# Expert outputs of a two-layer decoder on one Trainium2 core: interleaved activation parts, descending weights and PSUM columns

## The reference

```python
def block(xb):
    q = (xb @ w_pq).reshape(PEER_BLOCK, P_HEADS, 2, P_HALF)
    sc = jnp.einsum('thpc,hpkc->thpk', q, sub_keys)
    ...                                    # two top-16 lists per head -> 16 experts eid, their gates g
    ue = jnp.take(u_experts, eid, axis=0)
    ve = jnp.take(v_experts, eid, axis=0)
    a = jax.nn.gelu(jnp.einsum('thkd,td->thk', ue, xb), approximate=False)
    return jnp.einsum('thk,thkd->td', g * a, ve)
```

## Time and profile before

| what | value |
|---|---|
| median of 3 runs | 2074.11 us |
| profiled execution | 2075.4 us |
| its span, first to last instruction | 2073.7 us |
| granted TensorE clock, mean | 0.998 |
| TensorE matmuls busy | 2047.3 us, 99% of the span |
| VectorE, ScalarE, GpSimd busy | 1652.6, 1191.7, 343.5 us |
| first and last start of L1698 | 682.9 us, 2048.8 us, with other stages of layer 2 between |

### The profile page before, as it was taken

One profiled execution on the slowest core, in us unless ns is written; L12 is line 12 of the kernel. 1 busy time (PEld: TensorE's weight loads), 2 busy tenths in 40 slices (PEclk: granted clock), 3 DMA queues, 4 the chain that ended last, 5 costly groups with the idle time before them and its releaser, 6 DMA issues.

```text
span 2073.7 us, 38360 instructions
## 1 busy us (share of the span) xinstructions
PE 2047.3 (99%) x11544; PEld 1756.5 (85%) x11544; DVE 1652.6 (80%) x3041; ACT 1191.7 (57%) x1901; POOL 343.5 (17%) x342
## 2 busy tenths in 40 slices
PE   8999999999999999999999999999999999999998
PEld 6888888888888888888878888888888897888886
DVE  7786769999998677777788858799999986766666
ACT  6555556666666555555565545666766665555553
POOL 4010110000000333333340102000000003333331
PEclk9999999999999999999999999999999999999999
DMA  6445457776656877777653554577756568777773
GB/s 226 142 162 172 165 194 238 235 233 206 200 192 204 279 241 241 241 240 242 211 184 126 188 173 164 199 235 239 222 197 198 196 205 280 243 241 241 242 240 127
DMA packets 174249, 435.54 MB, mean 210 GB/s; under 512 B 19504, under 2 KB 85040, under 8 KB 173136
## 3 DMA queue, kind: packets, MB, share of 16 engines
q1 hardware_dynamic: 173520, 430.06, 63.4%
q0 software_dynamic: 640, 4.32, 0.6%
HBM read 397.60 MB, written 36.70 MB: 209 GB/s over the span
## 4 chain that ended last, share of the span: by engine, by line
PE 90%; DVE 5%; ACT 2%; DMA 2%; issue 1%; SPq 0%; POOL 0%; ACTq 0%; DVEq 0%
PE ps L1698 32%; PE ps L1317 31%; PE ps L1318 16%; PE ps L1673 3%; PE ps L1589 2%; DVE w_lo L835 2%; PE ps L1311 2%; DMA h_park<-h_out 1%; DMA raw<-slabs 1%; PE ps L1720 1%; ACT w_hi L712 1%; PE ps L1614 1%; PE ps L1648 1%; PE ps L1571 1%; DVE pick L1173 0%
## 5 line engine op out<-in xcount | busy, mean ns | idle before, releaser
L835 DVE TENSOR_TENSOR w_lo<-raw,w_hi 128x1024 fp32r<-128x1024 f32 x674 | 840.2, 1247 | 264.7 <-ACT w_hi L780 191.6
L1317 PE MATMUL ps<-act,w_hi 128*128 128x512 f32 x2784 | 986.2, 397 | 0.0
L1318 PE MATMUL ps<-act,w_lo 128*128 128x256 f32 x2784 | 777.2, 279 | 0.0
L1317 PEld LDWEIGHTS ps<-act,w_hi 128*128 128x128 f32 x2784 | 522.4, 188 | 117.4 <-issue 3.0
L1698 PE MATMUL ps<-w_hi,act 128*128 128x512 f32 x1936 | 596.5, 389 | 2.6 <-DVE act L1238 2.6
L1318 PEld LDWEIGHTS ps<-act,w_lo 128*128 128x128 f32 x2784 | 525.8, 189 | 0.1
L780 ACT ACTIVATE w_hi<-raw 128x1024 fp32r<-128x1024 f32 x248 | 263.1, 1061 | 325.0 <-PE ps L1698 313.3
L1698 PEld LDWEIGHTS ps<-w_hi,act 128*128 128x128 f32 x1936 | 363.5, 188 | 78.5 <-DVE act L1238 3.4
L1698 PE MATMUL ps<-w_lo,act 128*128 128x512 f32 x968 | 376.6, 389 | 0.0
L511 POOL TENSOR_TENSOR h_in<-h_in,gate 128x256 f32<-128x256 f32 x250 | 241.9, 968 | 444.3 <-DMA h_in<-h_park 444.1
L712 ACT ACTIVATE w_hi<-raw 128x1024 fp32r<-128x1024 f32 x248 | 261.1, 1053 | 0.0
(11 more groups left out here) (261 smaller groups left out, 1826.0 us busy)
## 6 DMA issues: line engine op xcount, KB each, us to landing
raw<-slabs SPq DMA_DIRECT2D x680, 512.0 KB, 4.2
h_park<-h_out SPq DMA_DIRECT2D x256, 128.0 KB, 2.1
h_in<-h_park SPq DMA_DIRECT2D x250, 128.0 KB, 3.9
memT<-mem POOLq DMA_DIRECT2D x2, 1024.0 KB, 5.6
skT<-sub_keys POOLq DMA_DIRECT2D x2, 1024.0 KB, 7.2
x_park<-xT SPq DMA_DIRECT2D x2, 1024.0 KB, 6.4
xT<-x_park SPq DMA_DIRECT2D x2, 1024.0 KB, 8.2
xT<-x SPq DMA_DIRECT2D x4, 256.0 KB, 5.5
```

Source lines behind the costliest of these rows:

```text
L835: nc.vector.tensor_tensor(w_lo[:, j].rearrange("p k c -> p (k c)"), raw[:, j, :], w_hi[:, j].rearrange("p k c -> p (k c)").bitcast(FP32), ...
L1317: nc.tensor.matmul(ps[:, j, :], w_hi[:, j, k, :], a[:, :, k, :], start=(k == 0), stop=False)
L1318: return nc.tensor.matmul(ps[:, j, hi * T:hi * T + T], w_lo[:, j, k, :], a[:, hi, k, :], start=False, stop=(k == KB - 1))
```

## The change

- The two parts of a gated tile are interleaved by element: `act_v[:, j, b, t, 0]` is the rounded part of token t, `act_v[:, j, b, t, 1]` its remainder. `act_v` begins 64 bytes (`PHASE`) after the start of `act_2`. A weight load therefore reads 128 columns at a distance of 8 bytes instead of 4. ScalarE and VectorE write at this step, and VectorE reads it.
- `h_in` and `y_nat` move behind `act_v`, and the tiles allocated after `act_2` start 512 bytes later. The large `gate` tile, which is aligned to 1024 bytes, keeps its address.
- In every matmul of the stage the moving weights are read from the last of the 512 columns to the first, and PSUM is written from the last column to the first, so each sum lands where it did.
- The early tiles keep their separate parts with adjacent elements; their matmuls have the descending weights and PSUM columns too.

The number of instructions on each engine, their order, sizes and semaphores are the same as before, and so are all DMAs.

```diff
+PHASE = 64
...
-        y_nat = [at(f"y_nat{b}", act_at + (2 * b + 1) * RING * T * 4, [P, 2, 512]) for b in range(TB)]
-        h_in = at("h_in", act_at + RING * T * 4, [P, RING, T])
+        act_v = at("act_v", act_at + PHASE, [P, RING, TB, P, 2], F32R)
+        h_at = act_at + 2 * RING * T * 4 + 512
+        top[0] += 512
+        y_nat = [at(f"y_nat{b}", h_at + b * RING * T * 4, [P, 2, 512]) for b in range(TB)]
+        h_in = at("h_in", h_at, [P, RING, T])
...
-                def gated_hi(g, j, hi=act_hi, h=h_in):
+                def gated_hi(g, j):
 
                     act.wait_ge(gated_ready, layer * V_SLABS + g * RING + j + 1)
-                    nc.scalar.activation(hi[:, j:j + 1, :], h[:, j:j + 1, :], ACT.Copy).then_inc(ga_hi_ready, 1)
+                    nc.scalar.activation(act_v[:, j, :, :, 0], h_in[:, j, :].rearrange("p (b t) -> p b t", b=TB),
+                                         ACT.Copy).then_inc(ga_hi_ready, 1)
...
-                def gated_lo(g, j, hi=act_hi, lo=act_lo, h=h_in):
+                def gated_lo(g, j):
                     dve.wait_ge(ga_hi_ready, layer * V_SLABS + g * RING + j + 1)
-                    nc.vector.tensor_tensor(lo[:, j:j + 1, :], h[:, j:j + 1, :], hi[:, j:j + 1, :].bitcast(FP32),
-                                            ALU.subtract).then_inc(ga_ready, 1)
+                    nc.vector.tensor_tensor(act_v[:, j, :, :, 1], h_in[:, j, :].rearrange("p (b t) -> p b t", b=TB),
+                                            act_v[:, j, :, :, 0].bitcast(FP32), ALU.subtract).then_inc(ga_ready, 1)
...
+                def tokens(j, b, part):
+                    return act_v[:, j, b, :, part]
+
+                def early_tokens(j, b, part):
+                    return (early_hi, early_lo)[part][:, j, b * P:(b + 1) * P]
...
-                            for i, (w, a) in enumerate(((w_hi, hi), (w_lo, hi), (w_hi, lo))):
-                                last = nc.tensor.matmul(ps[:, 2 * b + half, :], a[:, j, b * P:(b + 1) * P],
-                                                        w[:, j, 4 * half:4 * half + 4, :].rearrange("p k c -> p (k c)"),
+                            for i, (w, part) in enumerate(((w_hi, 0), (w_lo, 0), (w_hi, 1))):
+                                last = nc.tensor.matmul(ps[:, 2 * b + half, ::-1], of(j, b, part),
+                                                        w[:, j, 4 * half:4 * half + 4, :].rearrange("p k c -> p (k c)")[:, ::-1],
                                                         start=(first and i == 0), stop=(final and i == 2))
```

More of the change, by code:

```diff
@@ L763, in _, with early_gated_hi @@
                 assert n == GROUPS
-                def gated_hi(g, j, hi=act_hi, h=h_in):
+                def gated_hi(g, j):
                     act.wait_ge(gated_ready, layer * V_SLABS + g * RING + j + 1)
-                    nc.scalar.activation(hi[:, j:j + 1, :], h[:, j:j + 1, :], ACT.Copy).then_inc(ga_hi_ready, 1)
+                    nc.scalar.activation(act_v[:, j, :, :, 0], h_in[:, j, :].rearrange("p (b t) -> p b t", b=TB),
+                                         ACT.Copy).then_inc(ga_hi_ready, 1)
+                def early_gated_hi(j):
+                    act.wait_ge(gated_ready, layer * V_SLABS + j + 1)
+                    nc.scalar.activation(early_hi[:, j:j + 1, :], early_in[:, j:j + 1, :], ACT.Copy).then_inc(ga_hi_ready, 1)
                 for j in range(RING):
@@ L772, in _ @@
                     if j < EARLY:
-                        gated_hi(0, j, early_hi, early_in)
+                        early_gated_hi(j)
                     else:
@@ L1234, in _, with early_gated_lo @@
                     lo_part(layer, U_AT + TAIL_AT, 0, j)
-                def gated_lo(g, j, hi=act_hi, lo=act_lo, h=h_in):
+                def gated_lo(g, j):
                     dve.wait_ge(ga_hi_ready, layer * V_SLABS + g * RING + j + 1)
-                    nc.vector.tensor_tensor(lo[:, j:j + 1, :], h[:, j:j + 1, :], hi[:, j:j + 1, :].bitcast(FP32),
-                                            ALU.subtract).then_inc(ga_ready, 1)
+                    nc.vector.tensor_tensor(act_v[:, j, :, :, 1], h_in[:, j, :].rearrange("p (b t) -> p b t", b=TB),
+                                            act_v[:, j, :, :, 0].bitcast(FP32), ALU.subtract).then_inc(ga_ready, 1)
+                def early_gated_lo(j):
+                    dve.wait_ge(ga_hi_ready, layer * V_SLABS + j + 1)
+                    nc.vector.tensor_tensor(early_lo[:, j:j + 1, :], early_in[:, j:j + 1, :],
+                                            early_hi[:, j:j + 1, :].bitcast(FP32), ALU.subtract).then_inc(ga_ready, 1)
                 for j in range(RING):
@@ L1718, in _ @@
                         for b in range(TB):
-                            for i, (w, a) in enumerate(((w_hi, act_hi), (w_lo, act_hi), (w_hi, act_lo))):
-                                last = nc.tensor.matmul(ps[:, 2 * b + half, :], a[:, j, b * P:(b + 1) * P],
-                                                        w[:, j, 4 * half:4 * half + 4, :].rearrange("p k c -> p (k c)"),
+                            for i, (w, part) in enumerate(((w_hi, 0), (w_lo, 0), (w_hi, 1))):
+                                last = nc.tensor.matmul(ps[:, 2 * b + half, ::-1], tokens(j, b, part),
+                                                        w[:, j, 4 * half:4 * half + 4, :].rearrange("p k c -> p (k c)")[:, ::-1],
                                                         start=False, stop=(j == RING - 1 and i == 2))
```

6 lines of the change are left out of this document (3 added, 3 removed).

## The result

The changed kernel takes 2093.44 us (median of three runs, 2090.41 to 2095.98) where the kernel before takes 2074.11: a ratio of 1.0092, 95% interval 1.0068 to 1.0116. It is slower; I had forecast 2043 us. The new time lies inside the range of 2038 to 2110, on the side of rival 3.

A forecast was written before the change was run, and what follows sets the result against it. TensorE was taken as the bound, through the 226.4 ns pitch of 3072 expert-output matmuls. From 2075.4 us, -31.2 for the address relation and zeros elsewhere gave 2044.2, forecast as 2043 us because the runs' median is 1.3 lower; range 2038 to 2110.

The forecast's parts named there:

- rival 3: Expert-output matmuls: more collisions, the load touching twice as many memory lines; +10.4 ns x 3072, 2106 us; chance 0.13.
- The covers: Expert outputs: TensorE's 2.72 us a slab hides ScalarE's and VectorE's dearer strided work, at worst +0.40 and +0.41 us.
- The test on the early tiles: Early tiles walk down without interleaving: 227 ns there with 216 on main tiles credits interleaving; 216 there too credits direction.
- Address relation of the two reads: Expert outputs: new relation of weight load and moving read ends collisions; -10.4 ns on 3000 matmuls, -31.2 us.
- The excess over 216 ns: Expert outputs: 10.4 ns between the 226.4 ns pitch and L1571's 216, taken as collisions of load and moving reads.
- Near-equal speeds: Expert outputs: load at 9.2 bytes/ns and moving stream at 9.6, so their distance hardly changes and collisions end.
- Moving operand and PSUM columns downwards: Expert-output matmuls: descending read and write taken as 0, at most +205.6 ns x 3072, +632 us.
- Rival 1: Expert outputs: excess belongs to starting a full-rate stream, so the pitch stays 226.4 ns; 2074 us; chance 0.20.
- Rival 2: Expert outputs: descending stream taken at half rate at moving read or PSUM write, 432 ns a matmul; 2706 us; chance 0.09.

The follow-up runs named there:

- the interleaved kernel: Changed kernel with both walks turned upwards again, interleaved layout and its address kept; run beside the kernel before: 2086.76 us, ratio 1.0070.

## Why the prediction was wrong

**Right.** The bound is the pitch of 3072 matmuls, and nothing else moved the time: 3072 times the measured change of the pitch, 20.6 us, less some 3 us that the start gave back, is the stage's +17.3 us within half a microsecond. The covers held. VectorE is busy 223 and 217 of 300 us, the DMA engines 0.74 and 0.73, ScalarE's copy grew by 34 ns (I had allowed 400), the weight load's record by 5 ns (188 to 193), and TensorE waits for none of them. The test on the early tiles was the right one: they keep adjacent elements, they are at 233 ns, and this alone named the direction.

**The step that failed is "Address relation of the two reads", -10.4 ns on 3000 matmuls.** It has the wrong sign, and its reasoning falls in three places. The excess over 216 ns isn't made by collisions with the load: a load that reads one column, or half of them, doesn't end it, and a moving read of one column does. Near-equal speeds bring nothing: with the stream upwards the interleaved layout costs 3.3 ns. The changed kernel didn't even have that relation, since its load walks up while its stream walks down, so at these speeds their distance changes fastest of all; my sum took the speeds and left out the directions. And the load's address does count, but it only adds to the 226.7 ns that the kernel before already had at both of its load addresses; whether its place relative to the stream or its own place counts isn't separated. What I took for a loss to be recovered was the best that any kernel here reached at full clock for 512 different columns in one matmul.

**The second step that failed is the zero for "Moving operand and PSUM columns downwards".** Its bounds of 0 to +205.6 ns held the answer. PSUM's part is 0 (1325 matmuls), the moving operand's +6.7 ns (1288), and 6.7 x 3072 = 20.6 us is the whole result. I chose 0 by L1673, which skips elements of fp16 and walks up. That row says nothing of a descending read, and its skipping is no proof for fp32r either: there a step of two doubles the time of 256 columns (229.7 ns for 119.9). No row had a negative step: the honest value was unknown above zero, in the one resource that I had just named as full.

**The rivals.** Rival 3 is the nearest in time (2106, measured 2093) and wrong in mechanism: the walk down ends at 233.3 ns with every load tried. Rival 1's reading is right about the origin, as most of the excess goes with the moving read, and wrong in its conclusion that the stream's price doesn't change with its direction. Rival 2, a half rate, is excluded. The Trainium skill's rule that non-contiguous patterns slow the PSUM write (PSUM — Partial Sum Buffer, Specifications) doesn't extend to columns in descending order, as 1325 against 1325 shows.

**What stays open.** That the descending moving read costs the 6.7 ns is shown; why it does is not. Nor is it settled why 512 columns downwards end at 233.3 ns while 256 downwards run at 118.2, faster than upwards, near the beat of the loads, or what makes the load's places 0, 4, 64 and 128 good and 8, 32, 96 and 120 bad. 226.7 and 233.3 ns are steady distances; the 230 in between is a mean of changing ones (229 and 233 in the interleaved kernel). A weight load that itself walks down wasn't tried, and the moving read was never moved against a fixed load in small steps of four elements.

## What to carry to other kernels

Where fp32r matmuls of 512 columns run back to back at full clock, the moving read has no spare time: keep it ascending, contiguous and on a start that is a multiple of four elements, and choose the address of the stationary operand by measurement, since the difference between 226.7 and 233.3 ns can hang on it alone. The direction of the PSUM columns is free. Before you bet on an excess of a few ns, take the suspected cause away in one slot of the ring first, read the distance between starts and not the record's length, look at the granted clock beside every pitch, and don't carry a result from 256 columns to 512.

## What the runs showed that I had not expected

- A moving fp32r read at a step of two elements takes twice as long as an adjacent one: 256 columns 229.7 ns for 119.9, at full clock. At a step of four, 128 columns take 118 ns, where the loads' beat is near.
- Loads of 128 columns of 4 bytes start no closer than some 112 ns at full clock, even if their matmuls read a single column.
- The excess over the columns' own time, 13 ns for 512 adjacent ones, wasn't there at the 1.2 GHz level: 427 ns for 512 columns.
- A moving read that starts one element past a multiple of four takes 236 ns upwards and downwards, and 240 ns downwards at three elements past.
- The first two to three matmuls of a new form run at another pitch than the settled one (238 and 232 ns before 227), and up to nine do after some forms, so kernels that mix forms need more than a few of each.
- ScalarE's copy of 128 x 256 to every second fp32 element takes 435 ns instead of 401, 0.13 ns an element more.
